# Two blocks of a transformer with a batch of one: first scores of the second attention ahead of the last key unit, gate columns in another order, pooling rows normalised in pairs

## The reference

```python
h = _rmsnorm(x, g_pre[l]) * (1.0 + scale[:, None]) + shift[:, None]
proj = h @ w_in[l]
u_s, z_s, q_lat, kv_lat, k_rope, z_m, gl_s, gl_m = jnp.split(proj, split_at, axis=-1)
y_s = _ssm_branch(u_s, ...)                       # a state-space scan
glu_a, glu_b = jnp.split(jax.nn.gelu(y_s) @ w_glu[l] + b_glu[l], 2, axis=-1)
y_s = ((glu_a * jax.nn.sigmoid(glu_b)) * jax.nn.silu(z_s)) @ w_br_ssm[l]
y_m = _mla_branch(q_lat, kv_lat, k_rope, ...)     # the second attention, 16 heads
y_m = (y_m * jax.nn.silu(z_m)) @ w_br_mla[l]
merged = jax.nn.sigmoid(gl_s) * y_s + jax.nn.sigmoid(gl_m) * y_m
out = merged @ w_out[l]
x = x + gate[:, None] * _rmsnorm(out, g_post[l])
```

## Time and profile before

| | |
|---|---|
| median of 3 runs | 1366.47 us (1366.17 to 1367.79) |
| the profiled execution, its own time | 1370.41 us |
| its span (first to last instruction) | 1368.6 us |
| TensorE busy | 1283.5 us, 94% |
| VectorE busy | 1079.0 us, 79% |
| ScalarE busy | 633.2 us, 46% |
| GpSimd busy | 186.7 us, 14% |
| mean granted clock of TensorE | 0.983 |

### The profile page before, as it was taken

One profiled execution on the slowest core, in us unless ns is written; L12 is line 12 of the kernel. 1 busy time (PEld: TensorE's weight loads), 2 busy tenths in 40 slices (PEclk: granted clock), 3 DMA queues, 4 the chain that ended last, 5 costly groups with the idle time before them and its releaser, 6 DMA issues.

```text
span 1368.6 us, 26717 instructions
## 1 busy us (share of the span) xinstructions
PE 1283.5 (94%) x10588; PEld 1243.8 (91%) x10588; DVE 1079.0 (79%) x1692; ACT 633.2 (46%) x990; POOL 186.7 (14%) x205
## 2 busy tenths in 40 slices
PE   1999999899999999999998999999999898999996
PEld 1899999899999879999997889999999788999996
DVE  6898987798777768889876586999877786885674
ACT  3534444543444546543455453433455465355442
POOL 5598800000000000000002000000001110431000
PEclk9899999999999999999998999999999999999999
DMA  9898886399887459988833158997664488545551
GB/s 367 336 331 304 311 313 248 113 328 322 315 297 264 142 204 331 337 298 307 292 122 125 62 207 327 324 317 240 204 208 151 85 152 153 162 151 193 167 186 49
DMA packets 110893, 319.82 MB, mean 234 GB/s; under 512 B 24096, under 2 KB 35648, under 8 KB 110528
## 3 DMA queue, kind: packets, MB, share of 16 engines
q1 hardware_dynamic: 110784, 318.31, 68.7%
HBM read 313.26 MB, written 5.01 MB: 233 GB/s over the span
## 4 chain that ended last, share of the span: by engine, by line
PE 81%; DVE 7%; ACT 5%; DMA 3%; issue 2%; SPq 1%; ACTq 0%; DVEq 0%
PE tiles L375 17%; PE tiles L377 17%; PE tiles L376 17%; PE acc L375 7%; PE acc L376 7%; PE acc L377 7%; ACT w_hi L363 2%; DVE w_lo L367 2%; PE nrm L547 1%; DMA cons<-in_cons 1%; PE tiles L573 1%; PE acc L686 1%; PE tiles L575 1%; PE tiles L590 1%; DVE arena L1439 1%
## 5 line engine op out<-in xcount | busy, mean ns | idle before, releaser
L363 ACT CAST w_hi<-land 128x1024 fp32r<-128x1024 f32 x391 | 408.3, 1047 | 465.9 <-PE tiles L377 291.2
L367 DVE TENSOR_TENSOR w_lo<-land,w_hi 128x1024 fp32r<-128x1024 f32 x391 | 484.3, 1245 | 168.3 <-ACT w_hi L363 167.3
L375 PE MATMUL tiles<-x_hi,w_hi 128*128 128x256 f32 x1384 | 395.4, 286 | 7.4 <-ACT arena L1129 3.9
L377 PE MATMUL tiles<-x_hi,w_lo 128*128 128x256 f32 x1384 | 392.8, 284 | 0.0
L376 PE MATMUL tiles<-x_lo,w_hi 128*128 128x256 f32 x1384 | 392.8, 284 | 0.0
L375 PEld LDWEIGHTS tiles<-x_hi,w_hi 128*128 128x128 f32 x1384 | 266.8, 193 | 10.4 <-ACT arena L1129 4.4
L376 PEld LDWEIGHTS tiles<-x_lo,w_hi 128*128 128x128 f32 x1384 | 266.7, 193 | 0.1
L377 PEld LDWEIGHTS tiles<-x_hi,w_lo 128*128 128x128 f32 x1384 | 266.6, 193 | 0.0
L1394 DVE SCALAR_TENSOR_TENSOR arena<-arena 128x1024 f32<-128x1024 f32 x184 | 227.2, 1238 | 12.3 <-ACT arena L1152 9.1
L375 PE MATMUL acc<-h_hi,w_hi 128*128 128x256 f32 x704 | 199.4, 283 | 1.5 <-DVE h_lo L1413 1.5
L376 PE MATMUL acc<-h_lo,w_hi 128*128 128x256 f32 x704 | 199.2, 283 | 0.0
(11 more groups left out here) (341 smaller groups left out, 1648.7 us busy)
## 6 DMA issues: line engine op xcount, KB each, us to landing
land<-in_stream SPq DMA_DIRECT2D x391, 512.0 KB, 4.6
arena<-in_gstream SPq DMA_DIRECT2D x184, 512.0 KB, 6.5
w_dram<-arena SPq DMA_DIRECT2D x3, 512.0 KB, 6.5
arena<-w_dram SPq DMA_DIRECT2D x6, 256.0 KB, 9.5
arena<-in_c_rows SPq DMA_DIRECT2D x2, 512.0 KB, 6.4
x<-in_x_t SPq DMA_DIRECT2D x1, 1024.0 KB, 12.8
arena<-in_ssm_bn SPq DMA_DIRECT2D x1, 1024.0 KB, 7.6
u_dram<-arena SPq DMA_DIRECT2D x1, 1024.0 KB, 5.3
```

Of the source, the lines that this page charges most:

```text
L363: nc.scalar.copy(w_hi[:, u % RING], land[:, u % LAND]).then_inc(hi_done, 1)
L367: nc.vector.tensor_tensor(w_lo[:, u % RING], land[:, u % LAND], w_hi[:, u % RING].bitcast(F32), ALU.subtract).then_inc(lo_done, 1)
L375: nc.tensor.matmul(outs, lh, rh, start=first, stop=False, **kw)
L377: last = nc.tensor.matmul(outs, ll, rh, start=False, stop=end, **kw)
```

## The change

It has three parts.

1. Pooling. The first two quarters of block `G_POOL` are loaded ahead of the last FFN unit and worked off by VectorE ahead of the last `hidden` of the FFN; the third stays ahead of the reciprocal, the fourth comes after the rests. Products and rests come in pairs: two `norm_tile`, then their two `norm_lo`.
2. Second attention. TensorE runs `scores(0)` ahead of the last `kvup` unit; VectorE runs `scores_max(0)` ahead of the last two `q2_rope`, then `normalise(0)`, and `scores_max(1)` behind it. `normalise` is one product of 128x1024 with the four reciprocals broadcast, in place of four products of 128x256 with a scalar each.
3. Gates. The order is `zs`, `brm`, `glm`, `gls`. `brm` is read out of PSUM by ScalarE, `glm` goes through sigmoid into `gs_t`, and VectorE multiplies the two in SBUF. The eight `a_hi` of the attention's result move from ahead of the gates to behind the first two of them, four and four, and the `a_lo` likewise.

```diff
-          ("lat", 4), ("kr", 1), ("u", 6), ("qup", 4), ("kvup", 4), ("u2", 2), ("zm", 8), ("glm", 8), ("brm", 8),
-          ("zs", 8), ("gls", 8), ("glu", 16), ("brs", 8), ("out", 8)]
+          ("lat", 4), ("kr", 1), ("u", 6), ("qup", 4), ("kvup", 4), ("u2", 2), ("zm", 8), ("zs", 8), ("brm", 8),
+          ("glm", 8), ("gls", 8), ("glu", 16), ("brs", 8), ("out", 8)]
...
+                if f == 0:
+                    for q in range(2):
+                        g_load(G_POOL, q)
                 load_unit(sp, u, u % LAND)
                 if f == 0:
-                    g_load_block(G_POOL)
                     units("pool", 2)
+                    for q in range(2, 4):
+                        g_load(G_POOL, q)
...
                 scores(0)
+                between()
                 scores(1)
-                if beside:
-                    beside(-1)
+                beside(-1)
                 for g in range(groups):
                     n = n0 + g
                     sm, pt = ws[g % 2]
-                    pe.wait_ge(pn_done, 4 * (n + 1))
+                    pe.wait_ge(pn_done, n + 1)
...
             attention(0, 8, att2_tile, q2, k2, v2, QK_2, V_2, ws2, lambda g: (
-                pe.wait_ge(qrope_done, g + 1), pe.wait_ge(kb_done, 1), wait_freed(pe, TILE["kvup"] + 11)), beside)
+                pe.wait_ge(qrope_done, g + 1), pe.wait_ge(kb_done, 1), wait_freed(pe, TILE["kvup"] + (11 if g else 2))), beside,
+                      lambda: kvup_unit(3))
...
-            for n in range(KT):
+            def mla_hi(n):
                 act.wait_ge(af_done, 4 + n + 1)
                 nc.scalar.copy(a_hi[:, n], t_buf[:, n]).then_inc(ah_done, 1)
...
-                if nm == "glm":
-                    evacuate(o, tile_of(nm, n), mrg[:, n], ACT.Sigmoid)
-                elif nm == "zs":
+                if nm == "zs":
                     evacuate(o, tile_of(nm, n), zs_t[:, n], ACT.Silu)
-                elif nm == "gls":
+                elif nm == "brm":
+                    evacuate(o, tile_of(nm, n), mrg[:, n])
+                else:
+                    if nm == "gls":
+                        act.wait_ge(glm_done, n + 1)
                     evacuate(o, tile_of(nm, n), gs_t[:, n], ACT.Sigmoid)
                 ahead()
+                if i < 2:
+                    for k in range(4 * i, 4 * i + 4):
+                        mla_hi(k)
...
+                if f == 0:
+                    dve.wait_ge(base_done, 1)
+                    for q in range(2):
+                        g_part(G_POOL, q, "silu")
                 hidden(f, 21, 0, 0)
...
-            for q in range(2):
-                g_part(G_POOL, q, "silu")
+            g_part(G_POOL, 2, "silu")
             root(1)
-            norm_t(1)
+            for k in range(0, KT, 2):
+                for c in range(2):
+                    norm_tile(1, k + c, t_buf)
+                for c in range(2):
+                    norm_lo(1, k + c, t_buf, x_hi, x_lo)
             gate_coef(1, 40, vec("pool_scale", 0, 8))
-            for q in range(2, 4):
-                g_part(G_POOL, q, "silu")
+            g_part(G_POOL, 3, "silu")
...
-                for r in range(4):
-                    V.tensor_scalar(sm[:, r], sm[:, r], att_s[:, g % 2, 12 + r:13 + r], None,
-                                    ALU.mult).then_inc(pn_done, 1)
+                V.tensor_tensor(sm, sm, att_s[:, g % 2, 12:16].unsqueeze(2).to_broadcast([P, 4, T]),
+                                ALU.mult).then_inc(pn_done, 1)
...
             scores_max(0, 0, ws2)
+            ahead()
+            q2_rope(6)
+            q2_rope(7)
+            normalise(0, 0, ws2)
+            ahead()
             scores_max(1, 1, ws2)
-            ahead()
-            normalise(0, 0, ws2)
             ahead()
...
-                if nm == "brm":
-                    wait_tile(dve, TILE["brm"] + n)
+                if i < 2:
+                    for k in range(4 * i, 4 * i + 4):
+                        a_part(k, t_buf[:, k], 13 + k, al_done)
+                if nm == "glm":
                     wait_freed(dve, TILE["glm"] + n)
-                    V.tensor_tensor(mrg[:, n], tiles[:, (TILE["brm"] + n) % 2, 0:T], mrg[:, n],
-                                    ALU.mult).then_inc(freed["d"], 1)
+                    V.tensor_tensor(mrg[:, n], mrg[:, n], gs_t[:, n], ALU.mult).then_inc(glm_done, 1)
```

More of the change, by code:

```diff
@@ L116 @@
 HI_AT = {19: (0, 1, 2, 3), 26: (4, 5)}
-GATES = [(_name, _n) for _name in ("glm", "brm", "zs", "gls") for _n in range(KT)]
+GATES = [(_name, _n) for _name in ("zs", "brm", "glm", "gls") for _n in range(KT)]
 LAST = [(0, 4), (4, 6), (6, 8)]
@@ L312, in build_program @@
         y_done, gel_done, gv_done = sem("y_done"), sem("gel_done"), sem("gv_done")
-        zm_done = sem("zm_done")
+        zm_done, glm_done = sem("zm_done"), sem("glm_done")
         vs_done, zp_done = sem("vs_done"), sem("zp_done")
@@ L503, in _ @@
                     sp.dma_start(u2[r:r + 16], u_rows[g, t]).then_inc(u_in, 16)
-            for u in range(UNIT["zm"] + 6, UNIT["glm"] + 4):
+            for u in range(UNIT["zm"] + 6, UNIT["zs"] + 4):
                 load_unit(sp, u, u % LAND)
@@ L513, in _ @@
                     sp.dma_start(ba2[r:r + 16].rearrange("p j r n -> p j (r n)"), w_rows[g]).then_inc(ba_in, 16)
-            u = UNIT["glm"] + 4
+            u = UNIT["zs"] + 4
             for k in range(4):
-                while u < UNIT["glm"] + Y_AT[k] + 8:
+                while u < UNIT["zs"] + Y_AT[k] + 8:
                     load_unit(sp, u, u % LAND)
@@ L675, in _, with attention @@
             rot2 = cons[0:QK_2, CON["rot2"]:CON["rot2"] + QK_2]
-            def attention(n0, groups, tile, qq, kk, vv, parts, vdim, ws, ready, beside=None):
+            def attention(n0, groups, tile, qq, kk, vv, parts, vdim, ws, ready, beside, between):
                 def scores(g):
@@ L721, in attention @@
                     m.then_inc(part_done, 1)
-                    if beside:
-                        beside(g)
+                    beside(g)
             pe.wait_ge(one_in, 16)
@@ L932, in _, with kvup_unit @@
                     m.then_inc(used if pair else part_done, 1)
-            for n in range(4):
+            def kvup_unit(n):
                 u = UNIT["kvup"] + n
@@ L962, in _ @@
                                      stop=True).then_inc(qrot_done, 1)
+            for n in range(3):
+                kvup_unit(n)
             def beside(g):
@@ L1576, in _ @@
             ffn(0, 0, 3, 16, [*rng("pool", 0, 2), UNIT["ffn1"]], 1)
-            dve.wait_ge(base_done, 1)
-            for q in range(2):
-                g_part(G_POOL, q, "silu")
+            g_part(G_POOL, 2, "silu")
             root(1)
-            norm_t(1)
+            for k in range(0, KT, 2):
[3 more added lines that the diff above has]
+                    norm_lo(1, k + c, t_buf, x_hi, x_lo)
             gate_coef(1, 40, vec("pool_scale", 0, 8))
-            for q in range(2, 4):
-                g_part(G_POOL, q, "silu")
+            g_part(G_POOL, 3, "silu")
             blocks[0] += 1
@@ L1893, in _ @@
             ahead()
-            for n in range(KT):
-                a_part(n, t_buf[:, n], 13 + n, al_done)
             for i, (nm, n) in enumerate(GATES):
                 ahead()
-                if nm == "brm":
-                    wait_tile(dve, TILE["brm"] + n)
+                if i < 2:
+                    for k in range(4 * i, 4 * i + 4):
+                        a_part(k, t_buf[:, k], 13 + k, al_done)
+                if nm == "glm":
                     wait_freed(dve, TILE["glm"] + n)
-                    V.tensor_tensor(mrg[:, n], tiles[:, (TILE["brm"] + n) % 2, 0:T], mrg[:, n],
-                                    ALU.mult).then_inc(freed["d"], 1)
+                    V.tensor_tensor(mrg[:, n], mrg[:, n], gs_t[:, n], ALU.mult).then_inc(glm_done, 1)
                 if 2 <= i < 26 and i % 3 != 1:
@@ L2180 @@
         columns(w_in2[:, 2592:3616]),
+        columns(w_in2[:, 1024:2048]),
+        columns(a["w_br_mla_2"][0]),
         columns(w_in2[:, 4640:5664]),
-        columns(a["w_br_mla_2"][0]),
-        columns(w_in2[:, 1024:2048]),
         columns(w_in2[:, 3616:4640]),
```

## The result

The changed kernel takes 1358.18 us (median of 4 executions, 1357.42 to 1361.88), the kernel before 1367.13 (4 executions, 1366.17 to 1368.0). The ratio is 0.994, with a 95% interval of 0.9923 to 0.9957. So it is faster by 8.95 us in the medians, 5.9 to 10.5 by the interval. The forecast was 1352.7 and the range ended at 1358.0: the direction was right, and the size and, by a little, the range were wrong. The forecast counted from a median of 1366.47 (three executions), the comparison from 1367.13 (four), so the 0.2 us beyond the range are within the noise. The 4.9 us between a gain of 13.8 and one of 8.95 are not. The profiled execution of the changed kernel took 1361.88 us with a span of 1360.1, that of before 1370.41 and 1368.6. Time and span differ by 1.8 us in every execution, so all of the 3.9 us by which the profile of before exceeds its median lie inside the span.

A forecast was written before the change was run, and what follows sets the result against it. TensorE, busy 94% of the span, was taken as the bound, with gains only where it waits or runs at half clock; 4.8 + 1.8 + 5.7 + 0.3 + 1.2 = 13.8 us less gave median 1352.7, range 1349.5 to 1358.0.

The forecast's parts named there:

- Pooling: Pooling up to the norm's band: VectorE sets the pace, band at 247.65, full clock, 4.8 us less (3.5 to 5).
- Head of the attention: Second attention's start: mask wait goes, about 4.0 us wait and half clock return ahead of values(0); 1.8 us less.
- 0.3 us for GpSimd's first table step: Second attention's start: scores_max(1) on VectorE ends 0.3 us later because GpSimd's table step lies beside it.
- Rival 2: Second attention's start gives nothing: GpSimd makes product and split dearer by 1.0 us each; 1354.5 us, chance 0.14.
- bound by ScalarE at 7.3 us: Second attention, ahead of values(1): 7.3 us at full clock, set by ScalarE.
- Broadcast product: Second attention's division: 0.07 us more for each two heads, inside VectorE's 0.8 spare; last division 0.3 us less.
- Gates up to `state_in`: Gates: the 3.9 us wait for ScalarE's first tile and half clock behind it go; 5.7 us less (3 to 6).
- Against it I put 0.3 for eight products: Scan's last parts: glm times brm on VectorE costs 0.3 us against the 1.5 wait saved; 1.2 us less net.
- I cost that at nothing: Gates: VectorE's a_lo, splits and scan start come about 3.8 us later, free since state_out wants the scan four tiles later.
- the prediction's own signs of being wrong: TensorE waiting for the scan ahead of state_out, for x_lo over 1.5 us, or between attention and gates on a landing.
- rival 5: Gates and scan: VectorE's 3.8 us lag is never made up, four state_out pairs wait 5.2 each; 1373.5 us, chance 0.06.
- idle a fifth of the span: Argument against VectorE's lag staying through the scan: VectorE is idle a fifth of the span.

The follow-up runs named there:

- the run with the late products: Changed kernel with VectorE's eight products of glm and brm moved behind the scan parts that the third and last state_out pairs wait for: 1356.44 us, ratio 0.9916.

## Why the prediction was wrong in size

**Bound and method.** Right: TensorE's waits and its half clock account for nearly all that changed.

**Pooling.** Right. First group at 240.49 (forecast 240.5), the band at 247.52 (247.65), one long wait of 1.44 us (1.3), clock 1.00. The 4.90 of the pair is a little more than the mean: the band comes at 251.90 in the three profiles with the old pooling and at 247.38 in the eleven with the new one, 4.5 apart.

**Head of the attention: the step that failed is the 0.3 us for GpSimd's first table step, which "now lies beside it".** It is 1.7 (split 0.87, negation 0.84), shown by the run with the table step held back. The first values came 38.06 us after the first rotation; the forecast's 1086.7 against 1049.94 is 36.8. The order of the rest was as forecast: the wait of 4.3 us (4.0), ScalarE's queue as its cause, the half clock behind it. Rival 2 had named the mechanism and priced it at 2 us, but for the product and the split; it was the split and the negation that paid, and the product took 1.23. That the second values would be bound by ScalarE at 7.3 us was wrong too. The half clock made 8.52 of TensorE's 6.25, and the forecast's 7.3 with 1.4 for half clock gives 8.7: two errors that cancel, so this agreement is luck.

**Broadcast product.** Costed at nothing apart from 0.3 at the end. The end was right (0.33), but the head would be 1.9 us longer with the four products.

**Gates up to `state_in`.** Right, 5.65 for 5.7; no tile waits, as forecast.

**`brm` and scan: the step that failed is "Against it I put 0.3 for eight products" of `glm` and `brm`, together with "I cost that at nothing".** TensorE's wait for `brm` is gone, but VectorE with the scan then sets the pace ahead of the third and fourth pair: 22.6 and 21.9 us where TensorE's work alone is 20.6 (22.60 less 1.96). This is the first of the prediction's own signs of being wrong. Before, VectorE was idle for 2.5 of the 22.0 us between the second pair and the scan's last addition, which ended 0.3 us ahead of the third pair (1220.59 and 1220.93); now it needs 21.5 us for as many instructions, as its product of two tiles in SBUF, and the split ahead of it, are slow beside GpSimd, which the one that read PSUM was not. Between the third and the fourth pair five products come on top, where there was none, 21.6 busy of 21.8 us. By the runs the products cost 1.0 and 0.66 us at the two pairs, and GpSimd's table step 1.2 at the third. What VectorE's later start has in it, the 3.8 us costed "at nothing", stays open. This is the mechanism of rival 5 at a seventh of its size (3.2 us of waits, not 20.8), and what the text put against it, "idle a fifth of the span", is a mean over stages and says nothing about this one.

**The rest.** 2.04 of the 5.3 us between forecast and profile are the scatter of one stretch between executions, shown by fourteen profiles of it. Medians even part of that out. They differ by 7.6 to 8.95 us, where the stages without that stretch add up to 10.6. The pair overstates the pooling by 0.4. What else lowers the medians stays open.

## What to carry to other kernels

Ahead of moving an instruction on a queue that runs in order, ask of each instruction behind it which wait it inherits: the copy of the probabilities was ready 7 us before it ran. A wait that goes from TensorE uncovers the next engine, so take from the trace that engine's work between the same two points, not its mean share of the span. And compare stages by a few milestones in several profiled executions before a difference of 2 us is given a cause.

## What the runs showed of the hardware

An instruction of VectorE that worked in SBUF and began while one of GpSimd ran paid about the same whatever its size: 0.84 for 4 numbers (0.17 to 1.01), 1.1 for 128x256 (0.41 to 1.50), 0.87 for 128x1024 (1.22 to 2.09), and 3.7 for four in a row (1.14 to 4.87). One scan took 1.37 in place of 0.26 (in the run with the late products). The mask, which reads PSUM (1.21), and the maximum (1.22) paid nothing. The Trainium skill (GPSIMD Engine Reference, section "1. Specifications") names instructions with two SBUF inputs or in a 2-port mode as those that contend; these rows agree. They add that it is a cost for each instruction, so that few large ones are better than many small ones there.

The price is about one instruction of GpSimd, 1.07 us, and GpSimd pays in turn. These are its rows in the changed kernel beside the product of 1074.33 and the split of 1075.47:

```profile
1074.35 2.13 POOL L1980 TENSOR_TENSOR rope_tab<-base_t,chunk_t 128x512 f32<-128x512 f32 x1 [36.59 <-DVE arena L1835]
1076.56 1.93 POOL L1981 TENSOR_TENSOR rh<-base_t,chunk_t 128x512 f32<-128x512 f32 x1
```

The product began 0.02 us ahead of GpSimd's first and took its usual 1.23, and GpSimd's took 2.13; then the split took 2.09, and GpSimd's next 1.93. The starts and ends read as if each waits until the other's instruction is done. No run tests this by itself.

The half clock behind the wait of about 4 us cost between 1.5 and 2.5 us in five executions (7.77 to 8.76 us between first and second values, where 6.25 is full speed); behind the wait of 3.5 us, with the table step held back, it was 2.7 (8.97).
